# Where a few columns of dense work stand in the second layer's mixing

## Time and profile before

| what | value |
|---|---|
| median of 3 runs | 2865.04 us (2860.57 to 2866.55) |
| profiled execution, its own time | 2857.61 us |
| span of that execution | 2855.5 us |
| PE busy | 2791.9 us, 98% of the span |
| DVE busy | 1396.7 us, 49% |
| ACT busy | 738.0 us, 26% |
| mean granted clock of PE | 0.997 |

### The profile page before, as it was taken

One profiled execution on the slowest core, in us unless ns is written; L12 is line 12 of the kernel. 1 busy time (PEld: TensorE's weight loads), 2 busy tenths in 40 slices (PEclk: granted clock), 3 DMA queues, 4 the chain that ended last, 5 costly groups with the idle time before them and its releaser, 6 DMA issues.

```text
span 2855.5 us, 58645 instructions
## 1 busy us (share of the span) xinstructions
PE 2791.9 (98%) x25729; PEld 1820.4 (64%) x25729; DVE 1396.7 (49%) x2665; ACT 738.0 (26%) x1499; POOL 214.8 (8%) x184
## 2 busy tenths in 40 slices
PE   7999999999999999999999999999999999999999
PEld 3555555555644444847888544666666677787887
DVE  2666566665323233236778211766767633313541
ACT  3233343322222222103111002433333322311110
POOL 1000000000000002305445000000000000000000
PEclk9999999999999999999999999999999999999999
DMA  7111111111233333226543224211112133346554
GB/s 254 56 44 43 45 42 41 39 47 42 75 104 103 103 112 111 82 83 184 153 121 109 69 74 136 66 50 56 49 49 56 48 97 108 107 133 192 149 151 121
DMA packets 499998, 264.36 MB, mean 93 GB/s; under 512 B 42865, under 2 KB 493889, under 8 KB 499233
## 3 DMA queue, kind: packets, MB, share of 16 engines
q1 hardware_dynamic: 498016, 251.58, 30.3%
q0 software_dynamic: 1728, 9.03, 0.9%
HBM read 255.33 MB, written 5.24 MB: 91 GB/s over the span
## 4 chain that ended last, share of the span: by engine, by line
PE 91%; ACT 4%; DVE 4%; issue 1%; POOL 0%; DMA 0%; POOLq 0%; DVEq 0%; ACTq 0%
PE psum L504 45%; PE psum L1133 12%; PE psum L1244 8%; PE psum L525 2%; PE psum L744 2%; PE psum L972 1%; PE psum L866 1%; PE psum L852 1%; PE psum L565 1%; PE psum L960 1%; PE psum L950 1%; PE psum L835 1%; PE psum L902 1%; PE psum L694 1%; PE psum L734 1%
## 5 line engine op out<-in xcount | busy, mean ns | idle before, releaser
L504 PE MATMUL psum<-hT,strips 128*128 128x256 f32 (+1 forms) x3200 | 1108.0, 490 | 2.6 <-ACT arena L1725 2.1
L504 PEld LDWEIGHTS psum<-hT,strips 128*128 128x128 f32 x3200 | 579.8, 189 | 332.9 <-issue 274.1
L1244 PE MATMUL psum<-arena,strips 128*128 128x512 f32 (+1 forms) x704 | 227.6, 486 | 0.6 <-DVE arena L2731 0.6
L1244 PEld LDWEIGHTS psum<-arena,strips 128*128 128x128 f32 x704 | 133.7, 190 | 93.1 <-issue 83.2
L504 PE MATMUL psum<-arena,strips 128*128 128x256 f32 (+1 forms) x416 | 125.9, 461 | 0.9 <-DVE done L2582 0.9
L504 PEld LDWEIGHTS psum<-arena,strips 128*128 128x128 f32 x416 | 78.9, 190 | 45.0 <-issue 36.8
L2731 DVE SCALAR_TENSOR_TENSOR arena<-psum,mod,arena 128x256 f32<-128x256 f32 x24 | 10.9, 481 | 193.7 <-PE psum L1244 193.7
L2122 DVE TENSOR_SCALAR arena<-arena 128x512 f32<-128x512 f32 (+1 forms) x88 | 69.9, 795 | 69.5 <-ACT arena L1981 67.4
L1133 PE MATMUL psum<-arena,rwkv_branch 128*128 128x256 f32 x424 | 100.1, 381 | 0.0
L2517 DVE SCALAR_TENSOR_TENSOR arena<-arena,psum 128x256 f32<-128x256 f32 (+1 forms) x26 | 13.6, 523 | 162.6 <-PE psum L504 162.6
L1491 POOL COPY arena<-arena 128x512 f32<-128x512 f32 x16 | 9.7, 609 | 1086.7 <-DVE arena L2226 1086.7
(11 more groups left out here) (299 smaller groups left out, 4052.7 us busy)
## 6 DMA issues: line engine op xcount, KB each, us to landing
strips<-in_w_in_dram SPq DMA_DIRECT2D x152, 512.0 KB, 3.9
strips<-in_ada_w_dram SPq DMA_DIRECT2D x80, 512.0 KB, 4.9
strips<-in_ffn_up_dram SPq DMA_DIRECT2D x46, 512.0 KB, 3.8
strips<-in_ffn_down_dram SPq DMA_DIRECT2D x32, 512.0 KB, 4.0
conv_branch<-in_ffn_up_dram SPq DMA_DIRECT2D x28, 512.0 KB, 4.8
arena<-in_ada_w_dram SPq DMA_DIRECT2D x4, 2048.0 KB, 13.4
strips<-in_w_in_dram SPq DMA_DIRECT2D x32, 256.0 KB, 3.4
strips<-in_a_out_w_dram SPq DMA_DIRECT2D x16, 512.0 KB, 4.0
```

The costliest lines, as they stand in the source:

```text
L504: ins = mm(s.o[:, first:T], strip[:, b, k, :], rhs[:, k, first:T], k == 0, k == KT - 1)
L1244: ins = mm(s.o[:, lo:T], strip[:, b, j, :], hid[:, k, lo:T], k == 0, k == FT - 1)
```

## The change

Only PE's program changes. In the second layer (not `wide`), for a pair that has a next one (`ahead`):

- the fill after corner_below is 3 columns and no longer 5;
- through_inverse has a fill of 1 column ahead of lrb2 and one ahead of lrb3, where it had none;
- for the first pair alone, the second fill ahead of half_step is 11 columns and no longer 13, and the one after value_products is 4 and no longer 2.

In the first layer, the fill of 2 ahead of lrb2 stays, and the new one ahead of lrb3 is of 0 columns. The programs of the other engines stay as they are.

```diff
@@ -824,8 +824,8 @@
                     pe.wait_ge(*slots["t10", l, i].freed)
                     for m in range(4):
-                        if m == 2 and ahead and wide:
-                            fill(steps, 2)
+                        if m in (2, 3) and ahead:
+                            fill(steps, 2 if wide and m == 2 else 0 if wide else 1)
                         s = take(A, f"lrb{m}", l, i)
@@ -1087,7 +1087,7 @@
                     if lo and ahead:
-                        fill(steps, 8 if i else 13)
+                        fill(steps, 8 if i else 11)
                     if i > 0:
                         head_var(i - 1)
                     half_step(i)
@@ -1104,9 +1104,9 @@
                     value_products(i)
-                    fill(steps, 4 if wide or not ahead else 3 if i else 2)
+                    fill(steps, 4 if wide or not ahead else 3 if i else 4)
                     corner_below(i)
-                    fill(steps, 4 if wide or not ahead else 5)
+                    fill(steps, 4 if wide or not ahead else 3)
                     if ahead:
                         key_sums(i + 1)
                         gate_in(i + 1)
```

## The result

| | before | changed |
|---|---|---|
| median | 2865.01 us (4 runs, 2860.57 to 2866.55) | 2896.34 us (4 runs, 2893.21 to 2897.26) |
| profiled execution, its own time | 2857.61 us | 2896.37 us |
| span | 2855.5 us | 2894.4 us |
| mean granted clock of that execution | 0.997 | 0.989 |

The ratio is 1.0102 (95% interval 1.0090 to 1.0114), which on 2865 us is 29.2 us (25.8 to 32.7); the two medians lie 31.3 us apart. The forecast was 2883.6 us with a range to 2892.1; the direction was right, the size was not.

A forecast was written before the change was run, and what follows sets the result against it. TensorE, busy 2791.9 of 2855.5 us, was taken to bound the kernel. Pairs 12.7 plus first pair 2.6 gave 15.2 us; with 3.4 for the clock, 18.6 on 2865.04 made 2883.6 us, range 2872.5 to 2892.1.

The forecast's parts named there:

- What bounds the kernel, and the place: TensorE holds 91% of the chain, so its idle goes into the time; lrb1 waits there for ACT's gate copy.
- C late, ACT's queue behind it: After corner_below, C ends late, conv_gate and the gate copy run 1.39 us late; idle before lrb1 grows 0.62 to 2.67.
- conv_gate's new wait: Sign in the changed trace: conv_gate on ACT waits for PE's columns of C seven times, some 1.3 us each.
- the first rival: At lrb1 and L852 the waits go and the kernel is faster, 2858.5 us; chance 4%.
- Two columns between the blocks at 0.48 each: One column before lrb2 and one before lrb3 hide next to nothing and cost 0.96 us a pair.
- the 2.11 forecast: Cost of each of pairs 2 to 7: 2.35 us later on PE less 0.24 given back, 2.11 us.
- First pair, 2.56 us: In the first pair conv_gate and lrb1 start 1.84 us late; plus 0.96, minus 0.24, costs 2.56 us.
- The sum, 15.2 us: Loss over all seven pairs without the clock: 12.7 us for six pairs plus 2.6 for the first.
- The clock, 3.4 us from two falls in seven: Behind the seven enlarged idles at lrb1 the clock falls twice, 1.7 us each: 3.4 us, bounds 0 and 11.9.
- the case of all seven: Third rival: the clock falls in each enlarged wait at lrb1, 15.2 + 11.9 = 27.1 us, 2892.1 us; chance 10%.
- The state chain gives back 0.24 a pair: At L852, DVE's lead takes 0.24 us off PE's 0.32 us wait in each pair; bounds 0 to 0.32.
- the term for the pairs: Pairs 2 to 7 lose 2.11 us each through idle and columns at the inverse's blocks, 12.7 us in all.

The follow-up runs named there:

- lrb0 twice: The changed kernel with lrb0's 16 products done twice in the second layer: 2883.92 us, ratio 1.0069 to the kernel before.
- lrb0 three times: The changed kernel with lrb0's 16 products done three times in the second layer: 2894.32 us, ratio 1.0099 to the kernel before.
- columns only: The kernel before, corner_below keeping five columns, with the two columns behind gate_in moved ahead of lrb2 and lrb3: 2873.05 us, ratio 1.0030.
- first pair's part: The kernel before with only the first pair's fills changed (11 columns ahead of half_step, 4 after value_products): 2865.78 us, ratio 1.0005.
- gate first: The changed kernel with ACT's conv_gate moved behind gate_in in the second layer: 2871.94 us, ratio 1.0026 to the kernel before.
- C late: The kernel before with three columns after corner_below and four behind gate_in, none between the inverse's blocks: 2872.84 us, ratio 1.0033.
- lrb0 five times: The changed kernel with lrb0's 16 products done five times in the second layer: 2882.88 us, ratio 1.0068 to the kernel before.

## Why the prediction was wrong

By its own steps:

- *What bounds the kernel, and the place:* right. PE's idle went into the time, and it arose at lrb1.
- *C late, ACT's queue behind it:* right. The idle was worked out at 2.67 us and is 2.64, seven times; half_step's at 1.66, and is 1.59. conv_gate's new wait is 1.56 us against the 1.3 or so named. lrb1 starts 1.52 us late in its pair against 1.39. Moving conv_gate behind the gate took most of the loss away, and the first rival, that the edit works as its shape suggests, had nothing for it.
- *Two columns between the blocks at 0.48 each:* too small. They cost 1.36 together. A pair whose clock doesn't fall costs 2.64 us by the stages of the trace (0.57 less before key_sums, 0.08 and 3.39 more from there through the blocks, 0.26 back), against the 2.11 forecast.
- *First pair, 2.56 us:* too small as well. Key_sums starts 0.24 us later after half_step, as worked out (0.23), once the stop of 1.66 us and the low clock are taken off; 3.03 more from there through the blocks and 0.26 back make 3.0.
- *The sum, 15.2 us:* by these stages it should have been 18.8. The table has 15.5 at full clock, its lower bound, so the agreement of that figure with 15.2 proves little.
- *The clock, 3.4 us from two falls in seven:* this is the step that failed. It took 15.8 us by the table, and 10 to 13 if the stages' 18.8 are taken off 29.2 or 31.3. Both of its factors were too small. How often: the clock fell behind lrb1's idle in five of seven pairs of the changed kernel and in four of seven of the one without the first pair's part. The two idles of L525 in one trace gave one in two; over the twelve traces the clock fell at 15 of 24 of them. How much: a fall took 1.7 or 3.4 us by (1 - clock) × time, and the forecast knew only the first. And where: it also fell at half_step's wait of 1.59 us with the stop of 1.66 us behind it, and behind a stop of 1.27 us in the fifth pair; I had priced neither place. The seven falls in the changed kernel's pairs make 15.3 us so counted, 10.2 of it at lrb1, and the profiled execution of before had none there. The Trainium skill's warning (TensorE: Matmul & The Clock Gate, "HAM oscillation"), that waits repeated in a loop throttle the clock each time, was nearer to the truth than my two in seven, though its own case has waits of some 3 to 5 us and here five of seven fell at 2.64. I had given the case of all seven 10%. Even that, 11.9 us with seven falls at 1.7, would have stayed 4 us short of 15.8, since the falls elsewhere weren't in it.
- *The state chain gives back 0.24 a pair:* right (0.24 to 0.26).

So direction and mechanism of the wait were right. The term for the clock was 3.4 us where 10 to 15.8 were measured, and the term for the pairs fell short by 3 to 4.

## What to carry to other kernels

Filler work belongs ahead of the wait, not behind it (two columns ahead of lrb1 made this kernel 8.9 us faster): find the instruction that idles and what releases it, and check that the filler's own product isn't needed, in program order, by the engine that does the releasing. When an edit lengthens an idle of TensorE that recurs, price the idle twice: once as itself, and once for the clock; and take the clock's usual toll from all timed runs and not from one profiled execution. Useless matmuls in the idle are a cheap test of which part is which, and so is each half of an edit alone: if the halves don't add up to the whole, look at the clock.

## What the runs showed of the hardware

How often the clock fell behind the same wait, by its length, over the profiled execution of each kernel:

| idle ahead of lrb1 | kernels | falls behind it |
|---|---|---|
| 2.64 us | changed, without first pair's part | 9 of 14 |
| 2.18 us | lrb0 twice | 2 of 7 |
| 1.71 us | lrb0 three times | 2 of 7 |
| 1.35 to 1.92 us | columns only | 1 of 7 (the one of 1.92) |
| 0.62 to 1.05 us | before, first pair's part, gate first, C late, lrb0 five times | 0 of 35 |

Length alone doesn't decide it. At other places the clock fell behind stops of 0.93 us (lrb0 three times, L744), 0.97 (columns only, L815) and 1.00 (first pair's part, L744), and stayed up behind one of 1.59 (before, L744).

In the mixing a fall took 1.7 or 3.4 us by (1 - clock) × time and nothing between; behind lrb1's idle of the changed kernel the blocks took 1.5 to 1.6 or 2.9 us longer by it. Within a kernel the idle was the same to 0.02 us in all seven pairs (but for columns only), and whether the clock fell behind it wasn't.
